# Column sums of squares moved to VectorE adds in a two-layer trunk kernel, and two reordered weight steps

## The chip, the cores and the metric

The kernel runs on 1 core of one Trainium2 chip. The metric is the time of the whole program on the device in microseconds (us), the median over runs.

## The reference, cut to what matters

The reference computes two layers on x of 1024 tokens by 1024 channels, all in float32. Each layer is a mixer sub-layer and a channel mixer, and each of these reads its input through an RMS norm:

```python
def rms_norm(x, g):
    y = xf * lax.rsqrt(jnp.mean(xf * xf, axis=-1, keepdims=True) + EPS)
...
        h = modulate(rms_norm(x, norm1_g[l]), sh1, sc1)
        x = x + g1 * mixer_sublayer(h, ...)
        h = modulate(rms_norm(x, norm2_g[l]), sh2, sc2)
        f = swiglu(h, ...) if l % 2 == 0 else moe_swiglu(h, ...)
        x = x + g2 * f
```

shift, scale and gate (`sh`, `sc`, `g`) come from `silu(c) @ ada_w[l] + ada_b[l]`. So there are four norms: the first of layer 0 reads the input x; the other three ("the later norms") read an x that the kernel has just updated.

## The kernel before, in words

x is kept transposed: a tile of 128 channels (partitions) by 1024 tokens, eight such tiles k = 0 to 7, each in two halves of 512 tokens. A norm's mean of squares over channels is therefore a sum over the partitions of eight tiles. The kernel squares a 128x512 tile on ACT and lets TensorE multiply it with a 128x128 matrix of ones; eight such column sums accumulate in a PSUM bank for each half. These matmuls are plain float32, and the trace shows each as two records of 128x512. ACT takes the square root and DVE the reciprocal.

The large products use a split: weight and activation are each a rounded part (`hi`) and its remainder (`lo`), and `mm3` (L257 to L261) issues three matmuls for one product. A weight block goes by DMA (SP's queue) into `w_raw`, ACT rounds it to `w_hi` (`round_w`), and POOL subtracts to get `w_lo` (`rest_w`). Two buffers alternate. All engines are written out by hand as five instruction streams for each phase, with semaphores between them; a barrier ends each phase. The phases in order are, for a layer: front (first norm and input projections), attention, back (gates, branch products, then w_o), and the channel mixer (dense in layer 0; route, expert, combine in layer 1).

**Back phase, w_o part** (L1311 to L1331 on TensorE): eight blocks j = NGATE to NGATE+7, each two half-blocks of 24 matmuls of 128x512. DVE adds each half-block to x (L1567, "residual"), ACT squares it (`x_square`, L1397), TensorE sums it (`x_sum`, L1286). The sum of block k's half stands behind the half-block of block k+1, so 14 of a layer's 16 sums are issued inside the w_o loop and two behind it. The roots (L1414) are the last work of the phase. ACT's stream is `round_w(j)`, then the squares of block j-2. TensorE's next half-block into the same bank waits for the residual (`added`).

**Dense phase** (L1573): for each half of the tokens a lap of 22 "up" steps (w1 and w3, 48 matmuls a step) and 8 "down" blocks (w2) of three parts each (24, 24 and 18 matmuls). Beside each part DVE multiplies and reduces a piece of the next layer's `ada_w` (`ada_part`), which TensorE adds up with a small matmul (L1752). After the third part DVE adds the block to x (L1807), ACT squares it (L1654) behind the rounding of a later part, and TensorE sums it (`total`, L1718): the total of block j-1 stands behind block j, and the last total behind the loop.

**Front phase of layer 1**: SP issues `load(0)`, the eight tiles of x (tile k for k of 4 or more waits until tile k-4 has landed), `load(1)`, then small parameters and the rope tables. ACT issues `round_w(0)`, `round_w(1)` and then the h_hi roundings (L622). DVE's stream is `invert(0)`, then for n = 0 to 15 `scale(n)` (L730) and `rest(n-1)` (L738), with `invert(1)` ahead of `scale(8)`. TensorE's first block waits for `rest(k)` at each k.

**Front phase of layer 0 (the opening)**: DVE forms four parts of the ada product (`ada_part`, L815 to L819, semaphore `added`), TensorE sums them, and DVE then makes shift and scale and enters the same stream of `scale` and `rest`. ACT has rounded weight blocks 0 and 1 by then, and POOL subtracts them (L652) as soon as they are rounded. The first norm of layer 0 sums its squares on TensorE too (L522); the change leaves that one.

Of the kernel before, what the change touches and what calls it, by code (L numbers as in the profile page):

```python
# [31 lines left out]
P = 128  # L32
# [317 lines left out]
def front_phase(nc, m, a, l):  # L350
# [44 lines left out]
    with phase(nc, *names) as (block, s):  # L395
# [6 lines left out]
        def _(sp):  # L402
# [30 lines left out]
            if not first:  # L433
                load(1)
# [127 lines left out]
        def _(act):  # L562
# [53 lines left out]
            for j in range(2):  # L616
                round_w(j)
            for half in range(NHALF):
                for k in range(KT):
                    n = KT * half + k  # L620
                    act.wait_ge(s.scaled, n + 1)
# [27 lines left out]
        def _(pool):  # L649
# [15 lines left out]

            for j in range(3):
                rest_w(j)
# [368 lines left out]
def back_phase(nc, m, a, l):  # L1036
# [31 lines left out]
    x_sq = [m.place(f"x_sq{l}{b}", [P, HALF], F32, at) for b, at in enumerate((R + 138 * KB, R + 194 * KB))]  # L1068
# [14 lines left out]
    with phase(nc, "raw0", "raw1", "br0", "br1", "hi_ready", "lo_ready", "halves", "prods", "sig", "gated", "summed", "m_hi", "m_lo",  # L1083
               "x_in0", "x_in1", "added", "stored", "x_squared", "x_summed", "x_root",
# [79 lines left out]
        def _(pe):  # L1164
# [121 lines left out]
            def x_sum(k, half):  # L1286
                pe.wait_ge(s.x_squared, 2 * k + half + 1)
                if k == 0:
                    pe.wait_ge(s.r_root, 2)
                pe.matmul(m.ps[:, 6 + half, :], cst[:, K_ONE:K_ONE + P], x_sq[half][:, :], start=(k == 0), stop=(k == KT - 1)  # L1290
                          ).then_inc(s.x_summed, 1)

# [19 lines left out]
            for j in range(NGATE, NBACK):  # L1312
                b = j % 2
                pe.wait_ge(s.lo_ready, j + 1)
                for half in range(NHALF):
# [12 lines left out]
                    if j > NGATE:  # L1328
                        x_sum(j - NGATE - 1, half)
            for half in range(NHALF):  # L1330
                x_sum(KT - 1, half)  # L1331

        @block.scalar
        def _(act):
# [63 lines left out]
            def x_square(k, half):  # L1398
                act.wait_ge(s.added, 2 * k + half + 1)
                if k:  # L1400
                    act.wait_ge(s.x_summed, 2 * k + half - 1)
                act.activation(x_sq[half][:, :], m.x[:, k, toks[half]], ACT.Square).then_inc(s.x_squared, 1)
# [9 lines left out]
            for half in range(NHALF):  # L1412
                act.wait_ge(s.x_summed, 2 * KT - 1 + half)
# [4 lines left out]
        def _(dve):  # L1418
# [136 lines left out]
            if ada:  # L1555
# [4 lines left out]
                dve.wait_ge(s.folded, 2)  # L1560
            dve.wait_ge(s.x_in0, 16 * 6)
            for k in range(KT):
                if k == 6:
                    dve.wait_ge(s.x_in1, 16 * 2)
                for half in range(NHALF):
                    dve.wait_ge(s.halves, 2 * (NGATE + k) + half + 1)
                    dve.scalar_tensor_tensor(out=m.x[:, k, toks[half]], in0=m.ps[:, half, :], scalar=m.small[:, G1 + k:G1 + k + 1],  # L1567
                                             in1=m.x[:, k, toks[half]], op0=ALU.mult, op1=ALU.add).then_inc(s.added, 1)


def dense_phase(nc, m, a, l):
# [8 lines left out]
    sq = [m.place(f"f_sq{l}{b}", [P, HALF], F32, m.R + (176 + 6 * b) * KB) for b in range(2)]  # L1580
# [16 lines left out]
    with phase(nc, "squared", "summed", "root", "inv", "scaled", "hi", "lo", "raw0", "raw1", "hi_ready", "lo_ready", "mm_done",  # L1597
# [50 lines left out]
        def _(act):  # L1648
            def square(half, j):
                n = KT * half + j  # L1650
                act.wait_ge(s.added, n + 1)
                if n >= 2:
                    act.wait_ge(s.summed, n - 1)
# [902 lines left out]
```

## Time and profile before

| | |
|---|---|
| median of 3 runs | 5590.35 us (5587.02 to 5594.34) |
| the profiled execution's own time | 5590.09 us |
| its span | 5588.0 us |
| mean granted TensorE clock | 0.976 of full speed |
| TensorE busy | 5298.8 us, 95% of the span |
| VectorE busy | 2731.7 us, 49% |
| ScalarE busy | 1809.6 us, 32% |
| GpSimd busy | 757.4 us, 14% |

The profile shows one execution. PE is TensorE's matmul stream, PEld its weight loads, DVE VectorE, ACT ScalarE, POOL GpSimd, SP the engine whose queue issues the DMAs. Times in a timeline count from the start of the span. "[5.60 <-PE banks L261]" behind an instruction says that its engine sat idle for 5.60 us before it and what ended that. "x2" is two instructions merged into one row, whose duration is then that of both. L numbers are lines of the kernel before.

### The profile page before, as it was taken

To read this page: it belongs to the slowest core of one execution; us is meant where nothing else is said; L and a number is where in the kernel's file an instruction comes from. 1 tells how busy PE (TensorE), PEld (TensorE's weight loads), DVE (VectorE), ACT (ScalarE), POOL (GpSimd) and SP (SyncE) were. 2 spreads that over 40 slices of the span, in tenths; PEclk is the share of its full clock that TensorE was granted. 3 is DMA by queue.
4 is the path that set the end of the run, shared out by engine and by line. 5 is a ranking of instruction groups with operands and counts; after the bars stand their busy time and mean duration, and the time that the engine had idled before them with its cause. 6 is when DMAs were issued, how large, how long until landed. Compare 5 with 4: busy or idle time off the path is not lost. (4 is left out here: it accounts for less than half of the span.)

```text
span 5588.0 us, 71451 instructions
## 1 busy us (share of the span) xinstructions
PE 5298.8 (95%) x29668; PEld 4435.1 (79%) x29669; DVE 2731.7 (49%) x2494; ACT 1809.6 (32%) x1615; POOL 757.4 (14%) x329
## 2 busy tenths in 40 slices
PE   7998999999999899899995999999999999999995
PEld 5676667778788667676774989999899998898985
DVE  7344257333524632623323545445575457854566
ACT  3113121132222220412112333334463336643354
POOL 1411111134444232021111000000000000000001
PEclk9999999999999899999997999999999999999997
DMA  5211124333635512021124555555595558965578
GB/s 178 79 46 51 38 77 114 110 94 109 189 95 144 181 59 67 20 61 46 43 94 161 190 194 194 190 188 195 201 333 189 187 197 304 354 220 183 193 248 301
DMA packets 810515, 854.53 MB, mean 153 GB/s; under 512 B 19250, under 2 KB 732082, under 8 KB 809906
## 3 DMA queue, kind: packets, MB, share of 16 engines
q1 hardware_dynamic: 802274, 820.18, 45.2%
q0 software_dynamic: 4608, 16.78, 0.8%
q10 hardware_dynamic: 3408, 14.68, 0.8%
q8 instruction: 127, 2.08, 0.2%
q14 instruction: 98, 0.80, 0.0%
HBM read 793.90 MB, written 57.67 MB: 152 GB/s over the span
## 5 line engine op out<-in xcount | busy, mean ns | idle before, releaser
L259 PE MATMUL banks<-h_hi,w_hi 128*128 128x512 f32 x2432 | 993.6, 409 | 76.2 <-DVE h_lo L738 34.1
L259 PE MATMUL banks<-e_x_hi,e_w_hi 128*128 128x256 f32 x3584 | 1016.2, 284 | 14.5 <-DVE e_w_lo L2233 12.2
L260 PE MATMUL banks<-e_x_lo,e_w_hi 128*128 128x256 f32 x3584 | 1015.3, 283 | 0.0
L261 PE MATMUL banks<-e_x_hi,e_w_lo 128*128 128x256 f32 x3584 | 1015.1, 283 | 0.0
L260 PE MATMUL banks<-h_lo,w_hi 128*128 128x512 f32 x2432 | 957.0, 394 | 0.0
L261 PE MATMUL banks<-h_hi,w_lo 128*128 128x512 f32 x2432 | 956.8, 393 | 0.0
L2233 DVE TENSOR_TENSOR e_w_lo<-e_raw,e_w_hi 128x2048 fp32r<-128x2048 f32 x340 | 764.1, 2285 | 192.4 <-ACT e_w_hi L2171 190.7
L2171 ACT ACTIVATE e_w_hi<-e_raw 128x2048 fp32r<-128x2048 f32 x340 | 647.3, 1911 | 503.9 <-PE banks L261 491.4
L259 PEld LDWEIGHTS banks<-e_x_hi,e_w_hi 128*128 128x128 f32 x3584 | 689.1, 192 | 17.3 <-DVE e_w_lo L2233 14.0
L260 PEld LDWEIGHTS banks<-e_x_lo,e_w_hi 128*128 128x128 f32 x3584 | 689.1, 192 | 0.1
L261 PEld LDWEIGHTS banks<-e_x_hi,e_w_lo 128*128 128x128 f32 x3584 | 689.1, 192 | 0.0
L259 PEld LDWEIGHTS banks<-h_hi,w_hi 128*128 128x128 f32 x2432 | 462.2, 190 | 227.6 <-issue 59.8
L260 PEld LDWEIGHTS banks<-h_lo,w_hi 128*128 128x128 f32 x2432 | 463.3, 191 | 103.3 <-issue 12.9
L261 PEld LDWEIGHTS banks<-h_hi,w_lo 128*128 128x128 f32 x2432 | 462.4, 190 | 100.1
L2378 DVE TENSOR_TENSOR e_w_lo<-e_raw,e_w_hi 128x2048 fp32r<-128x2048 f32 x168 | 382.4, 2290 | 252.2 <-ACT e_w_hi L2178 252.1
L2178 ACT ACTIVATE e_w_hi<-e_raw 128x2048 fp32r<-128x2048 f32 x168 | 321.9, 1916 | 371.9 <-PE banks L261 371.9
L259 PE MATMUL banks<-e_w_hi,e_hid_hi 128*128 128x512 f32 x1120 | 436.8, 390 | 0.0
L261 PE MATMUL banks<-e_w_hi,e_hid_lo 128*128 128x512 f32 x1120 | 435.8, 389 | 0.0
L260 PE MATMUL banks<-e_w_lo,e_hid_hi 128*128 128x512 f32 x1120 | 435.8, 389 | 0.0
L253 POOL TENSOR_TENSOR w_lo<-w_raw,w_hi 128x1024 fp32r<-128x1024 f32 (+1 forms) x136 | 326.0, 2398 | 465.0 <-ACT w_hi L248 465.0
L2355 DVE TENSOR_TENSOR e_act<-e_act,banks 128x512 f32<-128x512 f32 (+1 forms) x168 | 100.4, 598 | 590.0 <-PE banks L261 550.3
L1150 POOL TENSOR_TENSOR w_lo<-w_raw,w_hi 128x1024 fp32r<-128x1024 f32 x80 | 191.5, 2394 | 1212.3 <-ACT w_hi L1339 1212.3
(307 smaller groups left out, 7043.3 us busy)
## 6 DMA issues: line engine op xcount, KB each, us to landing
e_raw<-in_moe_w_dram SPq DMA_DIRECT2D x510, 1024.0 KB, 5.9
w_raw<-in_ffn_w_dram SPq DMA_DIRECT2D x120, 512.0 KB, 3.9
w_raw<-in_w_in_dram SPq DMA_DIRECT2D x108, 512.0 KB, 4.1
f_ada_raw<-in_ada_w_dram SPq DMA_DIRECT2D x48, 512.0 KB, 5.0
g_ada_raw<-in_ada_w_dram SPq DMA_DIRECT2D x32, 512.0 KB, 4.1
e_io<-row_scratch SPq DMA_DIRECT2D x13, 1024.0 KB, 7.3
x_scratch<-x_res SPq DMA_DIRECT2D x24, 512.0 KB, 2.9
row_scratch<-stage SPq DMA_DIRECT2D x24, 512.0 KB, 2.6
```

What stands on the lines that cost most here:

```text
L253: pool.tensor_tensor(m.w_lo[b][:, 0:kt, :], m.w_raw[b][:, 0:kt, :], m.w_hi[b][:, 0:kt, :].bitcast(F32), ALU.subtract).then_inc(s.lo_ready, 1)
L259: pe.matmul(out, wh, rh, start=first, stop=False)
L260: pe.matmul(out, wh, rl, start=False, stop=False)
L261: return pe.matmul(out, wl, rh, start=False, stop=last)
L1150: pool.tensor_tensor(m.w_lo[j % 2][:, :, :], m.w_raw[j % 2][:, :, :], m.w_hi[j % 2][:, :, :].bitcast(F32), ALU.subtract).then_inc(s.lo_rea ...
L2171: act.activation(flat(w_hi[u]), flat(raw[n % RING]), ACT.Copy).then_inc(s.hi_ready, 1)
L2178: act.activation(flat(w_hi[c % 4]), flat(raw[n % RING]), ACT.Copy).then_inc(s.hi_ready, 1)
L2233: eng.tensor_tensor(flat(w_lo[u]), flat(raw[n % RING]), flat(w_hi[u]).bitcast(F32), ALU.subtract).then_inc(lo_sem[u], 1)
L2355: dve.tensor_tensor(act_t[h][:, 0:width], act_t[h][:, 0:width], m.ps[:, 2 + h, 0:width], ALU.mult).then_inc(s.hid, 1)
L2378: dve.tensor_tensor(flat(w_lo[c % 4]), flat(raw[n % RING]), flat(w_hi[c % 4]).bitcast(F32), ALU.subtract).then_inc(s.lo2, 1)
```

## The change: what it does, and the diff

In the back phases of both layers and in the dense phase, the square of the first tile goes into an accumulator, each later square into a scratch tile, and a new DVE operation `pile` adds it (128x512, float32, SBUF to SBUF). One float32 matmul with the ones for each half then takes the column sum of the accumulator. In the dense phase the sum of the first half is issued behind the first up step of the second half. In layer 1's front phase the load of the second weight block is issued behind x's fourth tile, and its rounding ahead of the sixth h_hi. In layer 0's front phase POOL waits for the four ada parts ahead of its first subtraction. The lists of semaphore names change with it (left out here).

```diff
@@ front_phase, sync @@
                         sp.wait_ge(x_in[k % 4], 16)
                     sp.dma_start(m.x[:, k, :], a.xs[P * k:P * k + P, :]).then_inc(x_in[k % 4], 16)
-            if not first:
-                load(1)
+                    if k == 3:
+                        load(1)
@@ front_phase, scalar @@
-            for j in range(2):
-                round_w(j)
+            round_w(0)
+            if first:
+                round_w(1)
             for half in range(NHALF):
                 for k in range(KT):
                     n = KT * half + k
+                    if not first and n == 5:
+                        round_w(1)
                     act.wait_ge(s.scaled, n + 1)
@@ front_phase, gpsimd @@
+            if first:
+                pool.wait_ge(s.added, NB)
             for j in range(3):
                 rest_w(j)
@@ back_phase @@
-    x_sq = [m.place(f"x_sq{l}{b}", [P, HALF], F32, at) for b, at in enumerate((R + 138 * KB, R + 194 * KB))]
+    x_acc = [m.place(f"x_acc{l}{b}", [P, HALF], F32, at) for b, at in enumerate((R + 138 * KB, R + 194 * KB))]
+    x_sq = [m.place(f"x_sq{l}{b}", [P, HALF], F32, R + at * KB) for b, at in enumerate((136, 140))]
@@ back_phase, tensor @@
-            def x_sum(k, half):
-                pe.wait_ge(s.x_squared, 2 * k + half + 1)
-                if k == 0:
-                    pe.wait_ge(s.r_root, 2)
-                pe.matmul(m.ps[:, 6 + half, :], cst[:, K_ONE:K_ONE + P], x_sq[half][:, :], start=(k == 0), stop=(k == KT - 1)
-                          ).then_inc(s.x_summed, 1)
...
-                    if j > NGATE:
-                        x_sum(j - NGATE - 1, half)
+            pe.wait_ge(s.r_root, 2)
             for half in range(NHALF):
-                x_sum(KT - 1, half)
+                pe.wait_ge(s.x_piled, 2 * (KT - 2) + half + 1)
+                pe.matmul(m.ps[:, 6 + half, :], cst[:, K_ONE:K_ONE + P], x_acc[half][:, :], start=True, stop=True).then_inc(s.x_summed, 1)
@@ back_phase, scalar @@
                 act.wait_ge(s.added, 2 * k + half + 1)
-                if k:
-                    act.wait_ge(s.x_summed, 2 * k + half - 1)
-                act.activation(x_sq[half][:, :], m.x[:, k, toks[half]], ACT.Square).then_inc(s.x_squared, 1)
+                if k >= 2:
+                    act.wait_ge(s.x_piled, 2 * (k - 2) + half + 1)
+                act.activation((x_sq if k else x_acc)[half][:, :], m.x[:, k, toks[half]], ACT.Square).then_inc(s.x_squared, 1)
@@ back_phase, vector @@
+            def pile(k, half):
+                dve.wait_ge(s.x_squared, 2 * k + half + 1)
+                if k >= 2:
+                    dve.wait_ge(s.x_piled, 2 * (k - 2) + half + 1)
+                dve.tensor_tensor(x_acc[half][:, :], x_acc[half][:, :], x_sq[half][:, :], ALU.add).then_inc(s.x_piled, 1)
...
                                              in1=m.x[:, k, toks[half]], op0=ALU.mult, op1=ALU.add).then_inc(s.added, 1)
+                    if k >= 2:
+                        pile(k - 1, half)
+            for half in range(NHALF):
+                pile(KT - 1, half)
@@ dense_phase @@
-    sq = [m.place(f"f_sq{l}{b}", [P, HALF], F32, m.R + (176 + 6 * b) * KB) for b in range(2)]
+    sq, acc = (m.place(f"f_{n}{l}", [P, HALF], F32, m.R + at * KB) for n, at in (("sq", 176), ("acc", 182)))
@@ dense_phase, scalar @@
                 act.wait_ge(s.added, n + 1)
-                if n >= 2:
-                    act.wait_ge(s.summed, n - 1)
-                act.activation(sq[n % 2][:, :], x_t[n % 2][:, :], ACT.Square).then_inc(s.squared, 1)
+                if j == 0 and half:
+                    act.wait_ge(s.summed, 1)
+                if j >= 2:
+                    act.wait_ge(s.piled, (KT - 1) * half + j - 1)
+                act.activation((sq if j else acc)[:, :], x_t[n % 2][:, :], ACT.Square).then_inc(s.squared, 1)
...
                 act.wait_ge(s.hid, FT * half + f + 1)
+                if half and f == 0:
+                    act.wait_ge(s.piled, KT - 1)
@@ dense_phase, tensor @@
-            def total(half, j):
-                n = KT * half + j
-                pe.wait_ge(s.squared, n + 1)
-                pe.matmul(m.ps[:, 6 * (1 - half), :], cst[:, K_ONE:K_ONE + P], sq[n % 2][:, :], start=(j == 0), stop=(j == KT - 1)
-                          ).then_inc(s.summed, 1)
+            def total(half):
+                pe.wait_ge(s.piled, (KT - 1) * (half + 1))
+                pe.matmul(m.ps[:, 6 * (1 - half), :], cst[:, K_ONE:K_ONE + P], acc[:, :], start=True, stop=True).then_inc(s.summed, 1)
...
                     up(half, f)
+                    if half and f == 0:
+                        total(0)
                 for j in range(KT):
                     down(half, j)
-                    if j:
-                        total(half, j - 1)
-                total(half, KT - 1)
+                if half:
+                    total(half)
@@ dense_phase, vector @@
                 dve.wait_ge(s.silu, n + 1)
+                if half and f == 1:
+                    dve.wait_ge(s.summed, 1)
...
+            def pile(half, j):
+                dve.wait_ge(s.squared, KT * half + j + 1)
+                if j >= 2:
+                    dve.wait_ge(s.piled, (KT - 1) * half + j - 1)
+                dve.tensor_tensor(acc[:, :], acc[:, :], sq[:, :], ALU.add).then_inc(s.piled, 1)
...
                     for q in range(NP):
                         ada_part(half, NP * j + q)
+                    if j >= 2:
+                        pile(half, j - 1)
                     residual(half, j)
+                pile(half, KT - 1)
```

## Rows read from the trace of the kernel before

**Rows 1.** The page: busy time of each engine, its share of the span and instructions.

```profile
PE 5298.8 (95%) x29668; PEld 4435.1 (79%) x29669; DVE 2731.7 (49%) x2494; ACT 1809.6 (32%) x1615; POOL 757.4 (14%) x329
```

**Rows 2.** Stretches: length, busy PE, PEld, DVE, ACT, POOL, PEclk, DMA, GB/s.

```profile
1039.40:1121.90 82.50, 82.50 (x340) 63.45 (x339) 9.76 (x13) 12.41 (x18) 11.99 (x5) 1.00 0.16 58
1416.89:1433.45 16.56, 16.56 (x76) 13.44 (x76) 11.45 (x7) 3.49 (x5) 7.25 (x3) 1.00 0.75 216
1905.50:1917.00 11.50, 0.00 (x0) 0.00 (x0) 3.85 (x3) 1.06 (x1) 2.34 (x1) 0.50 1.04 401
```

**Rows 3.** Timeline, DVE, layer 1's w_o blocks: start, us, engine, instruction.

```profile
2876.90 0.75 DVE L1567 SCALAR_TENSOR_TENSOR x_res<-banks,small,x_res 128x512 f32<-128x512 f32 x1 [4.62 <-PE banks L261]
2882.34 0.75 DVE L1567 SCALAR_TENSOR_TENSOR x_res<-banks,small,x_res 128x512 f32<-128x512 f32 x1 [4.69 <-PE banks L261]
2888.69 0.75 DVE L1567 SCALAR_TENSOR_TENSOR x_res<-banks,small,x_res 128x512 f32<-128x512 f32 x1 [5.60 <-PE banks L261]
...
2964.85 0.75 DVE L1567 SCALAR_TENSOR_TENSOR x_res<-banks,small,x_res 128x512 f32<-128x512 f32 x1 [5.59 <-PE banks L261]
```

**Rows 4.** Timeline, DVE, the dense stage's w2 blocks, first half.

```profile
1401.19 0.75 DVE L1807 SCALAR_TENSOR_TENSOR f_x<-banks,small,f_x 128x512 f32<-128x512 f32 x1 [3.32 <-PE banks L261]
...
1416.89 0.75 DVE L1807 SCALAR_TENSOR_TENSOR f_x<-banks,small,f_x 128x512 f32<-128x512 f32 x1 [4.17 <-PE banks L261]
```

**Rows 5.** Groups by form: one 128x512 sum or difference of two SBUF tiles on DVE.

```profile
L1791 DVE TENSOR_TENSOR hid<-f_hid,hid 128x512 fp32r<-128x512 f32 x44 | 30.5, 692 | 1.5
```

**Rows 6.** Timeline, all engines, end of layer 0's back phase.

```profile
1121.98 0.75 DVE L1567 SCALAR_TENSOR_TENSOR x_res<-banks,small,x_res 128x512 f32<-128x512 f32 x1 [5.59 <-PE banks L261]
1123.18 0.63 ACT L1402 ACTIVATE x_sq<-x_res 128x512 f32<-128x512 f32 x1 [5.99 <-PE banks L1290]
1123.82 1.28 ACT L1414 ACT_TABLE_LOAD   x1
1125.12 1.27 ACT L1414 ACTIVATE norm_root<-banks,const 128x512 f32<-128x512 f32 x2
1123.86 1.13 PE L1290 MATMUL banks<-x_sq,const 128*128 128x512 f32 x2 [0.20 <-ACT x_sq L1402]
```

**Rows 7.** Timeline, POOL and ACT: turn of the dense halves, and its end.

```profile
1518.69 4.67 POOL L253 TENSOR_TENSOR w_lo<-w_raw,w_hi 128x1024 fp32r<-128x1024 f32 x2 [9.70 <-ACT w_hi L248]
...
1899.30 0.63 ACT L1654 ACTIVATE f_sq<-f_x 128x512 f32<-128x512 f32 x1 [9.96 <-DVE f_x L1807]
1901.15 0.69 ACT L1658 ACTIVATE norm_rstd<-banks,const 128x512 f32<-128x512 f32 x1 [1.22 <-PE banks L1721]
```

**Rows 8.** Timeline, DVE, ACT and POOL, layer 1's first norm.

```profile
1908.30 3.31 DVE L730 SCALAR_TENSOR_TENSOR np_tmp<-x_res,small,norm_rstd 128x512 f32<-128x512 f32 x2 [2.26 <-DMA x_res<-x_scratch]
...
1921.38 2.33 DVE L738 SCALAR_TENSOR_TENSOR h_lo<-np_tmp,small,h_hi 128x512 fp32r<-128x512 f32 x1 [9.78 <-ACT h_hi L622]
...
1931.58 3.34 DVE L720 RECIPROCAL norm_rstd<-norm_rstd 128x512 f32<-128x512 f32 x1
...
1935.63 0.74 DVE L738 SCALAR_TENSOR_TENSOR h_lo<-np_tmp,small,h_hi 128x512 fp32r<-128x512 f32 x1
...
1919.68 1.06 ACT L567 ACTIVATE w_hi<-w_raw 128x1024 fp32r<-128x1024 f32 x1 [11.70 <-DMA w_raw<-in_w_in_dram]
...
1920.82 2.35 POOL L652 TENSOR_TENSOR w_lo<-w_raw,w_hi 128x1024 fp32r<-128x1024 f32 x1 [10.42 <-ACT w_hi L567]
```

**Rows 9.** Timeline, DVE and POOL, the opening of layer 0.

```profile
40.49 4.69 DVE L817 SCALAR_TENSOR_TENSOR ada_part<-ada_w,small,ada_part 128x512 f32<-128x512 f32 x6
...
46.39 8.83 DVE L817 SCALAR_TENSOR_TENSOR ada_part<-ada_w,small,ada_part 128x512 f32<-128x512 f32 x6
...
57.97 0.17 DVE L288 TENSOR_TENSOR small<-banks,small 128x16 f32<-128x16 f32 x1 [1.96 <-PE banks L543]
...
58.38 1.42 DVE L730 SCALAR_TENSOR_TENSOR np_tmp<-x_res,small,norm_rstd 128x512 f32<-128x512 f32 x2
...
47.22 5.09 POOL L652 TENSOR_TENSOR w_lo<-w_raw,w_hi 128x1024 fp32r<-128x1024 f32 x2 [46.79 <-ACT w_hi L567]
```

More of the change, by code:

```diff
@@ L1083, in back_phase @@
     with phase(nc, "raw0", "raw1", "br0", "br1", "hi_ready", "lo_ready", "halves", "prods", "sig", "gated", "summed", "m_hi", "m_lo",
-               "x_in0", "x_in1", "added", "stored", "x_squared", "x_summed", "x_root",
+               "x_in0", "x_in1", "added", "stored", "x_squared", "x_piled", "x_summed", "x_root",
                "gelu", "g_squared", "g_summed", "g_root", "g_inv", "g_normed", "g_turned", "vt_in", "mixed", "biased", "y2",
@@ L1412, in _ @@
             for half in range(NHALF):
-                act.wait_ge(s.x_summed, 2 * KT - 1 + half)
+                act.wait_ge(s.x_summed, half + 1)
                 act.activation(m.rstd2[:, half, :], m.ps[:, 6 + half, :], ACT.Sqrt, bias=cst[:, K_EPS:K_EPS + 1], scale=1.0 / D
@@ L1596, in dense_phase @@
     INV_STEP, H_STEP = 6, 7
-    with phase(nc, "squared", "summed", "root", "inv", "scaled", "hi", "lo", "raw0", "raw1", "hi_ready", "lo_ready", "mm_done",
+    with phase(nc, "squared", "piled", "summed", "root", "inv", "scaled", "hi", "lo", "raw0", "raw1", "hi_ready", "lo_ready", "mm_done",
                "silu", "hid", "hid_hi", "hid_lo", "x0", "x1", "added", "st0", "st1",
@@ L1651, in square @@
                 act.wait_ge(s.added, n + 1)
-                if n >= 2:
-                    act.wait_ge(s.summed, n - 1)
-                act.activation(sq[n % 2][:, :], x_t[n % 2][:, :], ACT.Square).then_inc(s.squared, 1)
+                if j == 0 and half:
[3 more added lines that the diff above has]
+                act.activation((sq if j else acc)[:, :], x_t[n % 2][:, :], ACT.Square).then_inc(s.squared, 1)
             def root(half):
-                act.wait_ge(s.summed, KT * half + KT)
+                act.wait_ge(s.summed, half + 1)
                 act.activation(m.rstd0[:, half, :], m.ps[:, 6 * (1 - half), :], ACT.Sqrt, bias=cst[:, K_EPS:K_EPS + 1], scale=1.0 / D
```

## The prediction, made before the changed kernel was run

> **What bounds the kernel now.** I read the page's busy times first: TensorE works for 95% of the span and no other engine for more than 49% [rows 1]. Shares don't say what a matmul fewer is worth, so next I read the stages that the change touches. In the w_o blocks the stretch is all TensorE: 82.50 of 82.50 us busy at full granted clock, DVE 9.76, ACT 12.41, POOL 11.99; in a dense w2 block it is 16.56 of 16.56 with DVE at 11.45 [rows 2]. Last, the timelines of the seams between phases, where TensorE idles and a chain over ACT, DVE, POOL and the DMAs sets the time. So sums inside a loop are paid on TensorE, and the rest on those chains.
>
> **Part 1, sums out of the w_o loops.** The distance of two residuals on DVE is one half-block of TensorE. Before the first sum it is 5.44 us (2882.34 - 2876.90), with a sum in it 6.35, and it stays so to the last: 13 x 6.35 from 2882.34 is 2964.85 [rows 3]. A sum costs 0.91. Of 14 sums issued in the loop the last stands behind the last half-block, beside the residual: 13 count. Two layers: 26 x 0.91 = **-23.7 us**.
>
> What comes in their place is one `pile` on DVE for each, 0.69 us by the nearest row of two SBUF inputs [rows 5]. It stands behind the residual that frees TensorE's bank, and DVE sits idle 5.6 us ahead of each residual, so it is free there. POOL's w_lo shares the stretch, and either may wait for the other by up to 2.4 us; both have over 3 us to spare. ACT's square now waits for the pile behind the same residual, and a weight rounding queued behind the square has most of a 10.9 us block left.
>
> **Part 2, the ends of the back phases.** Now: last residual 1121.98, square 1123.18 (held until then by the sum before it), table load to 1125.10, two roots to 1126.39 [rows 6]. After: residual to 1122.7, pile(6) to 1123.4, square to 1124.0 with pile(7, 0) beside it, pile(7, 1) to 1124.75, its sum of 1.13 (the two sums overlap by a little) to 1126.0, root to 1126.7. That is +0.3 each, **+0.6** for both. Bounds: 0, where the old wait of 0.45 hid more, and +2.0, three piles in a row with nothing given back.
>
> **Part 3, the dense phase.** A w2 block takes 15.70 us without a sum (1401.19 to 1416.89) [rows 4] and 16.56 with one [rows 2]: 0.86. Seven totals are issued inside a half's loop, of which the last stands beside the last residual; six count, in two halves: 12 x 0.86 = **-10.3**. The eighth of the first half is hidden today: TensorE has to wait there for the two weight blocks on which POOL works from 1518.7 to 1523.4 [rows 7]. Its successor stands behind an up step, where nothing idles: **+0.9**. DVE has 11.45 of a block's time in use [rows 2] and the pile makes it 12.1 of 15.7; it goes in front of the residual, where DVE idles 4.2 us [rows 4]. The new waits of silu and `hidden` on buffers are for work that ended a step earlier: nothing. At the end of the phase the chain square, total, root (1899.30 to 1901.84) [rows 7] gets a pile between square and total: **+0.7**, between 0.3 (if the store of x, issued with the square, is what the barrier waits for) and 1.2.
>
> **Part 4, layer 1's first norm.** DVE's first two scales end at 1911.61. The first `rest` comes only at 1921.38, since ACT's h_hi stands behind `round_w(1)`, which starts when its weights land, 1919.68 [rows 8]. With the rounding behind five h_hi, the first h_hi follows the first scale, and the first rest starts at about 1911.7. From the first rest to the eighth, on which TensorE's first block ends, it was 14.25 us (1921.38 to 1935.63), with one POOL subtraction that held DVE up (2.33 for 0.74) and one reciprocal (3.34) in it; without them seven tiles take 9.3, 1.33 each. The subtraction for block 1 now falls a few tiles later into the same stretch, so I keep 14.25: the eighth rest at 1925.95, 9.7 earlier.
>
> Of the queue: `load(1)` moves past four loads of x. At 401 GB/s [rows 2] a 512 KB load takes 1.3 us. x's first tile lands at 1908.3 [rows 8], so the last, eight loads later with the weights among them, at about 1918.8; DVE wants it at 1912.4 + 5 x 1.33 = 1919.0. That is tight but met. The worst case has a bound too: the same bytes had landed by 1919.68, so scale(7) starts then at the latest, and three operations of half a tile's 1.33, the reciprocal and a POOL hold of up to its whole 2.35 put the eighth rest at 1927.4: gain 8.2. The rounding of 1.06 in ACT's stream may delay the sixth rest by some tenths. I take **-9.2**, ends -8.2 and -9.7. The parameter loads behind keep their place and have 10 us and more.
>
> **Part 5, the opening.** Six ada operations take 4.69 us alone and 8.83 beside POOL's two subtractions (5.09) [rows 9]: 4.14 lost. After the change the parts end at 56.01 - 4.14 = 51.87; POOL then works to 56.96, while DVE's scale is ready at 58.38 - 4.14 = 54.24. Overlap 2.72, of which DVE lost 0.81 per us before: 2.2 lost, **-1.9** net. Ends: -4.1 (no hold) and -1.4 (held for all of it). TensorE's first block wants w_lo(0) at 54.4 and the first rest after 57, so DVE sets its start, as before.
>
> The Trainium skill ("SBUF — State Buffer", Who interferes with whom) has a rule on this: a DVE instruction with two SBUF inputs and a GpSimd one that reads SBUF exclude each other, and the later one is blocked for all of the earlier. By it this part would be 1.4 rather than 1.9, and the sum 0.5 us smaller. The rule speaks against the new piles as well, whose cover is stated above.
>
> **The sum.** -23.7 + 0.6 - 10.3 + 0.9 + 0.7 - 9.2 - 1.9 = -42.9 us. The profiled execution took 5590.09 by its own time (span 5588.0 and 2.1 around it), 0.3 below the median of 5590.35. So 5590.35 - 42.9 = 5547.4, given as 5547.
>
> **Rivals.**
> A. *The second weight block lands late after all.* If the DMA engines serve the open loads side by side, it may land with the last of them, 1919.68. The sixth h_hi then follows its rounding, the sixth rest starts at 1921.4, and two scales, a rest, the reciprocal and a hold later comes the eighth, at about 1929.5: 6 us instead of 9.2. With the opening at its lower end the sum is 3.7 less, 5551. For it: x's tiles and this load share one stretch of 401 GB/s [rows 2]. Against: x's first tile landed in its order, long before the last [rows 8].
> B. *Another engine paces the dense blocks.* Without the sum, the chain of ada loads and DVE pieces sets the block: part 3 gives nothing (-10.3 lost), 5558. For: DVE would be in use for 77% of a block. Against: the block of 15.70 had no sum and ran at TensorE's pace [rows 4].
> C. *A wait takes the sums' place; slower.* In the w_o loop pile(k-1) stands on DVE ahead of the next half's residual and waits for a square that stands on ACT behind `round_w`, which itself waits for TensorE to end a block. If that square came later than the next residual is due, over 5.44 us behind its own residual, TensorE would lose a half-block in each of the 14 blocks: 14 x 5.44 = 76, so 5590.35 - 42.9 + 76 = 5624. Against: the square starts 1.2 us behind its residual [rows 6], and its rounding waits only for the block that has just ended.
> D. *The sums were hidden.* Nothing but parts 4 and 5 comes, less the new chain pieces of 2.2: 5581. Against: 6.35 against 5.44.
>
> **How the numbers follow.** Forecast 0.81, A 0.10, B 0.06, D 0.02, C 0.01. With all terms at their best ends the forecast is 5544, with all at their worst 5551, where A lies too. The range adds 3 us below and 5 above, since the runs of before spread over 7 and the rules on who holds the port were read from few rows: 5541 to 5556; B, C and D lie outside. A measurement here tells about 0.2%, 11 us, from no change: faster is the forecast, A and B, 0.97; same 0.02 (D); slower 0.01 (C).
>
> **What the profile after would show.** Residuals 5.44 us apart all through w_o in both layers, w2 blocks 15.70 apart, TensorE full in both. 14 piles a layer in back and 14 in dense at about 0.69. The first h_hi of layer 1 right behind the first scale, the eighth rest some 14 us behind the first, and x's last tile no longer than tenths awaited. In the opening six ada operations at 4.69 in the fourth part, and a stretched first scale. Wrong would be: a residual with idle time put down to a pile or a square; POOL's w_lo stretched beyond what TensorE leaves, or ACT's rounding of layer 1's second block waiting for its load.

## The result, and the profile after

The changed kernel takes 5525.52 us (median of 4 runs, 5524.56 to 5527.48) against 5588.69 (4 runs, 5586.77 to 5594.34): ratio 0.9886, 95% interval 0.9874 to 0.9899, about 63 us faster. 5547 with a range of 5541 to 5556 was forecast. The sign was right, the amount was not: the kernel is 15 us below the low end, and no rival lies there either. The profiled execution took 5524.56 by its own time. One execution of the last experiment (e12) took 6323 us at a granted clock of 0.785, where all others have 0.972 to 0.979, and is left out.

The page's span, busy times, and the two queues that carry instructions (packets, MB, share):

```profile
span 5522.5 us, 71355 instructions
PE 5249.8 (95%) x29584; PEld 4413.2 (80%) x29585; DVE 2749.0 (50%) x2536; ACT 1810.1 (33%) x1615; POOL 756.5 (14%) x329
q8 instruction: 106, 1.74, 0.1%
q14 instruction: 42, 0.34, 0.0%
```

Against [rows 1] TensorE has 49 us less and VectorE 17 more. The page of before has for the two queues:

```profile
q8 instruction: 127, 2.08, 0.2%
q14 instruction: 98, 0.80, 0.0%
```

Twenty-one packets on q8 and 56 on q14 are gone with the change. At 0.2% of the DMA engines that looked like nothing, and it is the clue to what the forecast lacked.

**The stretches that the change edits** went as drawn. VectorE's timeline in layer 1's w_o blocks, then in layer 0's w2 blocks:

```profile
2848.50 0.75 DVE L1572 SCALAR_TENSOR_TENSOR x_res<-banks,small,x_res 128x512 f32<-128x512 f32 x1 [4.69 <-PE banks L261]
2853.94 0.75 DVE L1572 SCALAR_TENSOR_TENSOR x_res<-banks,small,x_res 128x512 f32<-128x512 f32 x1 [4.69 <-PE banks L261]
2859.38 0.75 DVE L1572 SCALAR_TENSOR_TENSOR x_res<-banks,small,x_res 128x512 f32<-128x512 f32 x1 [4.69 <-PE banks L261]
2860.05 0.68 DVE L1564 TENSOR_TENSOR x_acc<-x_acc,x_sq 128x512 f32<-128x512 f32 x1
2864.82 0.75 DVE L1572 SCALAR_TENSOR_TENSOR x_res<-banks,small,x_res 128x512 f32<-128x512 f32 x1 [4.09 <-PE banks L261]
...
1399.01 0.75 DVE L1821 SCALAR_TENSOR_TENSOR f_x<-banks,small,f_x 128x512 f32<-128x512 f32 x1 [4.11 <-PE banks L261]
1410.45 0.69 DVE L1828 TENSOR_TENSOR f_acc<-f_acc,f_sq 128x512 f32<-128x512 f32 x1
1414.71 0.75 DVE L1821 SCALAR_TENSOR_TENSOR f_x<-banks,small,f_x 128x512 f32<-128x512 f32 x1 [3.57 <-PE banks L261]
```

The residuals stay 5.44 us apart with a pile between them, where [rows 3] has 6.35; the w2 blocks are 15.70 apart (16.56 in [rows 2]), and each residual still waits for TensorE.

**The expert phase**, of which no line was changed, is where the rest came from. It works in a loop over items, each up to 256 rows (tokens) of one expert; an item with at most 128 rows takes the narrow branch of the loop, another the wide one. An item is counted here from ScalarE's first rounding of its rows. The first starts at 3048.3 before and 3003.9 after, 44.4 us earlier: up to here the total of 42.9 holds (its parts less well, see below). From the first item's start to the last's it is 2425.2 us before and 2405.6 after, 19.6 less, and the stretch behind is 1.5 shorter: 44.4 + 19.6 + 1.5 = 65.5, the difference of the spans. From one start to the next a long item (the wide branch) takes 241.3 before and 240.2 after, a narrow one 169.5 and 165.6. VectorE's waits in that phase, before and then after (total us, times, longest):

```profile
DVE e_act L2355 <- PE banks L261: 550.3, 140, 8.6
DVE e_act L2355 <- issue: 28.7, 4, 8.3
```

```profile
DVE e_act L2378 <- PE banks L261: 571.9, 148, 6.0
```

"issue" is a wait for nothing that the profile shows. One of the four, on VectorE's timeline of before, with what it does to TensorE on the second line:

```profile
3316.78 0.69 DVE L2355 TENSOR_TENSOR e_act<-e_act,banks 128x512 f32<-128x512 f32 x1 [8.33 <-issue]
...
3321.35 0.38 PE L259 MATMUL banks<-e_x_hi,e_w_hi 128*128 128x256 f32 x1 [0.84 <-DVE e_w_lo L2233]
```

After the change the same operation comes as soon as TensorE allows:

```profile
3275.44 0.69 DVE L2378 TENSOR_TENSOR e_act<-e_act,banks 128x512 f32<-128x512 f32 x1 [5.24 <-PE banks L261]
```

And the instruction queues' packets from the first item's start to the last's, before, then after:

```profile
q8 instruction: 25, 0.41, 0.1%
q14 instruction: 59, 0.48, 0.1%
```

```profile
q8 instruction: 6, 0.10, 0.0%
q14 instruction: 5, 0.04, 0.0%
```

The items are a loop. In the kernel after, the packets in it are about one fetch of its instructions (six of 16.4 KB on q8, where TensorE's loop has 1730 instructions); in the kernel before there are four times as many on q8 and twelve times on q14.

### The profile page after: what moved, and what is told of

Same layout as the page of the kernel before. It is cut to its first block and busy times, and to the rows that moved or that the text cites. A ratio compares the mean times of both kernels' runs of the same rounds, so it can differ in the third digit from the quotient of the medians.

```text
span 5522.5 us, 71355 instructions
## 1 busy us (share of the span) xinstructions
PE 5249.8 (95%) x29584; PEld 4413.2 (80%) x29585; DVE 2749.0 (50%) x2536; ACT 1810.1 (33%) x1615; POOL 756.5 (14%) x329
## 3 DMA queue, kind: packets, MB, share of 16 engines
q1 hardware_dynamic: 802274, 820.18, 45.7%
q8 instruction: 106, 1.74, 0.1%
## 5 line engine op out<-in xcount | busy, mean ns | idle before, releaser
L259 PEld LDWEIGHTS banks<-e_x_hi,e_w_hi 128*128 128x128 f32 x3584 | 688.9, 192 | 11.1 <-DVE e_w_lo L2256 10.9
```

Of the source, the lines that this page charges most:

```text
L259: pe.matmul(out, wh, rh, start=first, stop=False)
```

## The experiments

The theory: the change makes VectorE's stream 78 instructions longer ahead of the expert loop (counted in the compiled program; the trace shows them as 42 operations and 36 waits) and TensorE's 170 shorter, so the loops begin at other places within the blocks in which instructions are fetched. Rivals: the 20 us are the clock's, another engine's, or come from the data path that was changed. The tool is a wait that always holds already, put where its engine idles: it changes no result and no order, and only lengthens the stream (two such waits make one instruction in most places; 166 of them made 78).

**Move VectorE's loop alone.** The edit in the kernel before, in `hidden` of the dense phase (166 waits over its 44 calls):

```diff
                 dve.tensor_tensor(hid_lo[f], ...).then_inc(s.hid_lo, 1)
+                for _ in range(166 * (FT * half + f + 1) // (NHALF * FT) - 166 * (FT * half + f) // (NHALF * FT)):
+                    dve.wait_ge(s.hid, 2)
```

> The kernel before with 166 waits on VectorE that never hold (hid at 2, which it has from the start), spread over its 44 hidden blocks of the dense phase. They make 78 instructions, so VectorE's loop of the expert phase begins at its instruction 2058, as in the changed kernel, and not at 1980; TensorE's stays at 11621 and ScalarE's at 1581. Theory (the 20 us more than forecast come from where VectorE's expert loop lies in its instruction stream: it is fetched again every round): the expert phase becomes 20 us shorter, to intervals of 240.2 us for the long items instead of 241.3, the 8.3 us waits of VectorE at its line 2355 go, and the time is 5589 - 20 = 5569 (5565 to 5573). Rival (TensorE's or ScalarE's place in their streams, or the clock, or the layer-1 data path): 5589, intervals as before. Rival (the waits themselves cost): over 5589.

Measured 5570.38 us (6 runs) against 5591.04 for the kernel before beside it: 20.7 us less, ratio 0.9968 (0.9955 to 0.998, which is 11 to 25 us), by idle instructions alone. The packets of the first item to the last's:

```profile
q8 instruction: 25, 0.41, 0.1%
q14 instruction: 5, 0.04, 0.0%
```

Q14 is down to the 5 of the changed kernel and q8 where it was. No wait of VectorE in the items is put down to "issue" any more. The long items take 240.2 us, but two of them, in the later half, 241.6.

The same edit with 354 waits in the changed kernel puts the loop back:

> The changed kernel with 354 such waits on VectorE (178 instructions), so that its expert loop begins at 2236 = 1980 + 256, the place of before within a block of 256 instructions; everything else as in the changed kernel. Theory (VectorE's place modulo 256 decides): the expert phase gets its 20 us back, long items at 241.3 us, total 5525.5 + 20 = 5545 (5541 to 5550). Rival (another engine or the clock): 5525.5.

Measured 5549.34 us (4 runs), long items 241.1 to 241.4, 59 packets on q14 in the items, and 45.7 us of "issue" in front of VectorE's `e_act`: 24 us lost, the other direction of the same effect.

**Which block size.** The waits now stand at the head of the expert phase, beside the wait for its first rows (100 of them, 256 in the second kernel):

```diff
             dve.sem_inc(s.y_in, 1)
+            for _ in range(100):
+                dve.wait_ge(s.hid, 2)
```

> The changed kernel with 100 waits on VectorE that never hold, at the head of the expert phase (50 instructions, beside its wait for the first rows): its expert loop begins at 2108 = 1980 + 128. The DMA table gives 8 KB to a packet of the instruction queue that VectorE shares (0.34 MB in 42), so blocks of 128 instructions, if one has 64 bytes. Theory (the place within a block of 128 decides): slow as in the kernel before, about 95 packets on that queue, long items 241.2 us, 5525.5 + 21 to 24 = 5547 to 5549. Rival (blocks of 256): the place is one that neither kernel has had, and nothing says that it is slow; 5525.5 if it is not.

> The same with 256 waits (128 instructions), loop at 2186 = 2058 + 128. Theory (blocks of 128): as the changed kernel, about 42 packets, 5525.5 (within 3). Rival (blocks of 256): another place than the changed kernel's, and so a loss of up to 24 us.

Measured 5550.57 us with 50 instructions more and 5528.34 with 128 more. A shift by 128 changes nothing but 2.9 us in the first item (175.2 for 172.3, the waits themselves), and one by 50, which is before's place plus 128, brings all of it back (25 us, a little over what was expected). So a shift by 128 instructions leaves the place as good as it was, which agrees with the 8 KB of a packet on q14. A period of 64 would fit these shifts as well; none of the runs rules it out.

**The other engines.**

```diff
                 act.activation(act_t[f % 2][:, :], ..., ACT.Silu).then_inc(s.silu, 1)
+                if half == 0 and f < 5:
+                    for _ in range(2):
+                        act.wait_ge(s.hid, 2)
...
                     pe.wait_ge(s.lo, KT * half + KT)
+                for _ in range(2):
+                    pe.wait_ge(s.hid, 2)
```

> The changed kernel with waits that never hold on TensorE (44 instructions, two waits ahead of each up block) and ScalarE (5 instructions), so that both engines' expert loops begin where they did before (11621 and 1581), and VectorE's stays where the change put it (2058). Theory (VectorE's place alone): 5525.5, at most 1 to 2 us more for the 44 instructions on TensorE. Rival (TensorE's or ScalarE's place): the 20 us come back, 5545.

Measured 5572.38 us (6 runs), 47 more than the changed kernel, far outside both. The expert loop did it, on TensorE itself:

```profile
3258.19 0.39 PE L261 MATMUL banks<-e_w_hi,e_hid_lo 128*128 128x512 f32 x1
3264.88 0.58 PE L259 MATMUL banks<-e_x_hi,e_w_hi 128*128 128x256 f32 x1 [6.30 <-issue]
```

Once in each long item TensorE stands for 6.3 to 6.7 us with nothing to wait for, and then works at a lower clock for some us. The six us behind this stall and the six after those (length, then PE, PEld, DVE, ACT, POOL busy, then the granted clock, DMA share, GB/s):

```profile
3264.88:3270.88 6.00, 6.00 (x33) 6.00 (x34) 4.49 (x2) 1.93 (x2) 0.00 (x0) 0.61 1.04 324
3270.88:3276.88 6.00, 6.00 (x51) 5.90 (x51) 0.00 (x0) 3.68 (x3) 0.00 (x0) 1.00 0.93 292
```

33 matmuls where 51 fit: of the 9 us by which these items are longer (249 us), over 2 are the clock and the rest the stall. The queue q8 has 73 packets in the items:

```profile
q8 instruction: 73, 1.20, 0.2%
q14 instruction: 5, 0.04, 0.0%
```

My expectation said that the 44 instructions put TensorE's loop where it lay before. They did not: I had counted a matmul as one instruction. The page counts 84 matmuls fewer for 42 sums taken away, so an fp32 sum is executed as two, each with its weight load, and counts four; counted so, before and after differ by 170, not 44, and this kernel has a place of its own. That q14 stays at 5 clears ScalarE, whose place was before's here, and in e1 too.

With the count mended, TensorE's loop alone, by waits where it waits anyway, for the router's input and for the expert phase's first rows:

```diff
             pe.wait_ge(s.w_in, 32)
+            for _ in range(80):
+                pe.wait_ge(s.w_in, 32)
...
             pe.sem_inc(s.mm_done, 4)
+            for _ in range(260):
+                pe.wait_ge(s.mm_done, 4)
```

> The changed kernel with TensorE's expert loop moved by 170 instructions to 159 modulo 256, where it lies in the kernel before and in e1; VectorE's stays at 2058. Theory (in e1 two items were 241.6 instead of 240.2 us, so TensorE's place of before costs 2.8 us, and VectorE's the rest of the 20): about 127 packets on TensorE's queue, two or three items of 241.6 us, 5525.5 + 2.8 and at most 3 for waits that do not fit: 5528 to 5532. Rival (the place as counted does not decide): 240.2 us throughout and 106 packets.

Measured 5537.31 us (5 runs), above the 5528 to 5532 expected, since the waits cost 8 us and not at most 3: they made TensorE stand 46.9 us for the rows where it is 38.9 otherwise; of the rest, 3.5 are two long items of 242.0 and 241.9 (in each TensorE stands 1.4 to 1.5 us with nothing to wait for), with 25 packets on q8, as before and in e1. So of before's expert phase TensorE's place costs 3 us and VectorE's 17; the stretch behind, where TensorE waits 15.8 us for `c_diag` before, 16.0 in e2 and 15.8 in e5, but 13.6 in every kernel with VectorE's loop at the other place, goes with VectorE's place too.

| kernel | VectorE, mod 128 | TensorE, mod 256 | q14, q8 packets in all | first to last item, us | time, us |
|---|---|---|---|---|---|
| before | 60 | 159 | 98, 127 | 2425.2 | 5588.7 |
| e1 | 10 | 159 | 42, 127 | 2408.5 | 5570.4 |
| e2 | 60 | 245 | 100, 106 | 2426.8 | 5549.3 |
| e5 | 60 | 245 | 99, 106 | 2424.4 | 5550.6 |
| e6 | 10 | 245 | 43, 106 | 2408.5 | 5528.3 |
| after | 10 | 245 | 42, 106 | 2405.6 | 5525.5 |
| e11 | 10 | 159 | 42, 127 | 2410.0 | 5537.3 |
| e9 | 10 | 245 | 42, 107 | 2406.7 | 5555.4 |
| e10 | 10 | 245 | 42, 107 | 2405.9 | 5542.7 |
| e4 | 10 | 245 | 43, 106 | 2405.6 | 5534.7 |
| e12 | 10 | 245 | 42, 106 | 2405.9 | 5525.7 |
| e3 | 10 | 33 | 43, 173 | 2451.6 | 5572.4 |
| e7 | 10 | 45 | 42, 174 | 2456.1 | 5616.0 |
| e8 | 10 | 17 | 42, 107 | 2406.6 | 5550.7 |

The places are where the loop begins in the compiled stream, from an origin of my own; the differences between kernels agree with the instructions that the traces show. The time of e12 is the median of three executions.

**Each part undone.** The front phase's part (load and rounding of the second weight block as in before; no count changes):

```diff
-                    if k == 3:
-                        load(1)
+            if not first:
+                load(1)
...
-            round_w(0)
-            if first:
-                round_w(1)
+            for j in range(2):
+                round_w(j)
...
-                    if not first and n == 5:
-                        round_w(1)
```

> The changed kernel without the part for layer 1's first norm: the second weight block's load is issued ahead of x again, and its rounding stands ahead of the eight first halves. No engine's instruction count changes. Theory as forecast (the sixth to eighth rests come 9.2 us earlier by the change): 5525.5 + 9 = 5534.5 (5533.7 to 5535.2). Rival (the traces show a gain of 7.8 us in this phase, of which 3.8 are lost again before attention's end): 5529 to 5533.

Measured 5534.73 us (4 runs), 9.2 more. That it is the forecast to the tenth is chance: the four runs lie between 5529.17 and 5537.11, and the profiled ones of the two kernels are 4.6 apart.

The whole function of the back phase is before's again (14 column sums more in each layer, no piles), with waits as above at the head of the expert phase (396 on TensorE, 104 on VectorE), first with a place of TensorE's that I had miscounted:

> The changed kernel with the whole back phase of before (all 16 column sums of the w_o stretch in each layer), and waits that never hold at the head of the expert phase, in TensorE's 38 us wait for the rows and VectorE's beside it, so that TensorE's expert loop keeps its place modulo 256 instructions (a matmul counted as two, its weight load and its product) and VectorE's is at 2058. Forecast of the parts: 26 sums at 0.91 us less two ends at 0.3 = 23.1, so 5548.6 (5547.5 to 5550). Rival D (the sums were hidden): 5525.5. Rival (part of the 20 us is the sums' doing after all): over 5552.

Measured 5616.0 us (4 runs). Sums cannot explain it, the table does: TensorE's loop at 45, items of 250 us. 5525.5 + 23.1 for the sums + 50.5 in the items + 15.7 by which the idle waits outlast the wait for the rows (54.4 for 38.7) is 5614.8. With the place right (284 waits on TensorE, 80 of them at the router):

> As e7 (the whole back phase of before in the changed kernel), with TensorE's place now counted as the instructions are executed: an fp32 product takes two matmuls and two weight loads (the page counts 84 matmuls fewer for the 42 column sums taken away), so each counts four. By that count TensorE's expert loop of the changed kernel lies at 245 modulo 256, before's and e1's at 159, e3's at 33 and e7's at 45 (the two that lost 6.3 us in every long item), e8's at 17. Here it is at 245 again, VectorE's at 2058. Theory: no fetch stalls, about 107 packets on TensorE's queue, long items 240.2 us; the time is the forecast's 5525.5 + 23.1 = 5548.6 (5547 to 5551). Rival D (sums hidden): 5525.5. Rival (e7's 5616 came from the sums, not from the place): over 5600.

Measured 5555.36 us (5 runs), items 240.2. TensorE's wait for the rows, 5.1 longer than its 38.7:

```profile
3037.84 2.58 PE L2268 MATMUL banks<-const,e_io 128*128 128x128 f32 x11 [43.80 <-issue]
```

Less these 5.1 it is 5550.3, so the part is worth 24.8 (forecast 23.1), from five runs that lie between 5549.7 and 5562.8. The 5555.36 itself is above the 5547 to 5551 expected.

The dense phase's function as before, with 456 and 52 waits, then 400 and 52 with TensorE's split between router and rows (e8 happened to get a harmless place, but too many waits):

> The changed kernel with the whole dense phase of before, and waits that never hold at the head of the expert phase so that both expert loops keep their places. Forecast: 12 x 0.86 - 0.9 - 0.7 = 8.7, so 5534.2 (5533.5 to 5535.5). Rival (the dense phase gained 10 to 12 us by the traces, since the granted clock was 0.93 instead of 1.00 in a stretch of before): up to 5537 if that clock belongs to the sums and comes back with them, else as forecast.

> As e8 with TensorE's loop at 245 modulo 256; its waits that never hold are split between the router's wait (40 instructions) and the wait for the rows (160), since e8 showed 228 of them at the second place to take 57.7 us where the wait was 39.0, 18.7 us too long. Theory: 5534.2 plus 1 to 3 for waits that do not fit (5533.5 to 5538), long items 240.2 us. Rival: the dense phase gives more than the 8.7 us forecast, 5537 to 5541.

Measured 5550.66 and 5542.65 us; less the 18.7 and 11.4 by which the waits outlast the wait for the rows, 5532.0 and 5531.3: the part is worth 6 rather than 8.7, though runs of e10 from 5539.5 to 5545.6 hardly tell the two apart. Both medians are above what was expected, and above their rivals, because of the waits.

The opening:

```diff
-            if first:
-                pool.wait_ge(s.added, NB)
             for j in range(3):
                 rest_w(j)
```

> The changed kernel without the wait that puts the opening's remainders behind its parts. VectorE's and TensorE's places unchanged. Forecast of that part: 1.9 us (1.4 to 4.1); the trace shows 2.5 us at the first rest. So 5527.4 to 5528.0. Rival (the part gained nothing that lasts, since the front phase's stretches at a lower clock swallow it): 5525.5.

The three times are 5524.60, 5525.69 and 5531.12 us: they can't tell 2 us. Its timeline can, at the spot: the first rest starts at 59.53 us, and at 57.39 in the changed kernel, 2.1 earlier. Whether that lasts to the end is not shown.

## Why the prediction was wrong, and where it was right

**The step that failed** is in the sum: it took each edit's own stretch and let all else stand, so the expert phase and what follows it entered at nothing, without a reason, where the runs show about 20 us. The prediction read "the stages that the change touches" and no other. But the change lengthens VectorE's stream and shortens TensorE's, and the expert loop behind them is sensitive to where it lies. That is 20 us, shown from both sides by e1 and e2 (20.7 and 24) and split by e11. Nothing about the sums or piles enters: e1 has none of the change. The forecast's total for the parts, set on a kernel with the changed kernel's places, comes out: e1's 5570.4 less TensorE's 3 less 42.9 is 5524.5; measured 5525.5. That the place fell well was luck: e3 is the changed kernel with 44 idle instructions of TensorE's and loses 47.

It could have been suspected from the trace of before: 59 packets of instructions in a loop of 292 on VectorE, and 28.7 us of "issue" in front of one of its operations. How much the change would turn it, and which way, no row told, so such a case belongs in the range as a rival to either side.

**That the total came out so well is partly luck too.** Stretch by stretch, from VectorE's timelines of the two profiled executions:

| start of | before | after | gained since the row above |
|---|---|---|---|
| layer 0, first w_o residual | 1031.02 | 1026.19 | 4.8 |
| layer 0, last w_o residual | 1121.98 | 1105.28 | 11.9 |
| first w2 residual of half 0 | 1401.19 | 1383.31 | 1.2 |
| last w2 residual of half 0 | 1516.25 | 1493.51 | 4.9 |
| first w2 residual of half 1 | 1783.46 | 1758.71 | 2.0 |
| last w2 residual of half 1 | 1898.52 | 1868.82 | 5.0 |
| layer 1, first w_o residual | 2871.53 | 2837.69 | 4.1 |
| layer 1, last w_o residual | 2964.85 | 2919.22 | 11.8 |
| first item | 3048.3 | 3003.9 | -1.2 |

The rows of w_o and w2 are what the forecast said. The first row gains 4.8 where 1.9 was forecast, the turn of the dense halves 2.0 where it should lose 0.9, and the stretch with layer 1's norm 4.1 where 8.5 was due. These are stretches in which the granted clock changes from kernel to kernel: the eleven kernels that share the changed kernel's code up to layer 0's first w_o residual reach it between 1023.1 and 1031.9.

The Trainium skill ("Runtime: NRT & Kernel Launch", Instruction fetch mechanics) says that instructions are prefetched in sequence, in blocks of 16 KiB (256 instructions), into a memory that holds 512 of them (2048 on TensorE), and that a taken branch to a target outside the current window of two blocks stalls for a fetch. Stalls at a loop are what the runs show, the 6.3 us of e3 among them. The size agrees for TensorE (1.74 MB in 106 packets, 16.4 KB) but not for VectorE: its packets have 8 KB (0.34 MB in 42), and e6 finds a shift of 128 instructions harmless. By the page's sizes VectorE's loop of 292 instructions would fit into 512 and TensorE's of 1730 (both branches of an item) into 2048. At the places 245 and 17 TensorE's does (5 to 7 packets in the items); at 33 and 45 it is fetched over and over, and so is VectorE's at the place 60. What rule tells the bad places from the good ones is open.

**Part 1** (-23.7). From the first residual to the last, layer 0 took 90.9 to 91.0 us in the four kernels with the sums in the loop and 79.1 in the changed one, 11.9 less (up to 80.0 in others, with stretches at a lower clock); layer 1 93.3 in before and e1 (93.0 in e7 and e9) and 81.5 in the changed kernel, 11.8 less: 23.7. Right.

**Part 2** (+0.6). Layer 0: last residual to the last root's end 4.77 us, and 4.41 by [rows 6]: +0.36, as drawn. Layer 1 lost 2.1 up to the router's first product. TensorE stands 2.14 us for the last pile, the granted clock falls, and the two sums take 3.33 us for 1.95; in e4, the same code, it doesn't fall. Of the ten profiled executions with this end, layer 1's last residual to the last root's end takes 6.1 to 6.5 us in seven and 4.78 in three (e4, e8, e12); before has 4.12. The windows (length, then PE, PEld, DVE, ACT, POOL busy, then the clock), of the changed kernel, then the stretch of e4 that answers to the last:

```profile
2911.30:2918.30 7.00, 7.00 (x32) 5.81 (x31) 1.35 (x2) 0.63 (x1) 0.00 (x0) 1.00 0.01 2
2918.30:2921.30 3.00, 0.88 (x4) 0.39 (x4) 1.95 (x3) 0.63 (x1) 0.00 (x0) 1.00 0.17 70
2921.30:2925.30 4.00, 3.33 (x4) 0.91 (x4) 0.69 (x1) 2.58 (x3) 0.00 (x0) 0.57 0.19 79
```

```profile
2926.40:2930.40 4.00, 1.95 (x4) 0.65 (x4) 0.94 (x2) 2.66 (x3) 0.29 (x1) 1.00 0.20 81
```

0.57 is the lower of the two levels, 1.2 GHz, for most of the stretch. The forecast priced the wait and not this: +0.4 and +2.1 are 2.5 for both layers, over the bound of +2.0. Up to the first item 1.2 of layer 1's 2.1 are left.

**Part 3** (-8.7 net). The eight w2 blocks of a half take 110.2 and 110.1 us from residual to residual where they took 115.1: 9.8 less of the 10.3, the rest at a lower clock (e7 and e9 have 109.9 in the first half, the full 5.16 less). The total behind the up step costs 0.8 against e10, which has before's dense phase (265.2 for 264.4 from the last w2 residual of one half to the first of the other), but before itself takes 267.2 there. The first 20 us of that turn have a granted clock of 0.83 in before, 0.91 after and 1.00 in e10; the last 20 have 0.92, 1.00 and 0.91:

```profile
1756.25:1776.25 20.00, 17.66 (x73) 14.14 (x72) 11.40 (x10) 3.45 (x4) 6.78 (x4) 0.92 0.46 128
```

```profile
1733.51:1753.51 20.00, 17.66 (x80) 14.33 (x79) 11.37 (x10) 3.45 (x4) 6.61 (x3) 1.00 0.47 132
```

The end costs 0.7, on these two rows of ScalarE:

```profile
1869.61 0.63 ACT L1665 ACTIVATE f_sq<-f_x 128x512 f32<-128x512 f32 x1 [9.96 <-DVE f_x L1821]
1872.18 0.69 ACT L1669 ACTIVATE norm_rstd<-banks,const 128x512 f32<-128x512 f32 x1 [1.94 <-PE banks L1733]
```

2.57 from square to root, and 1.85 in [rows 7]. So 8.3 in its own stretches against e10 and 11.1 against before; by the times of e8 and e10 only 6 arrive. From the phase's last residual to the first of layer 1's w_o the changed kernel takes 968.9 us and e10 964.0, and by windows of 40 us its clock is 0.91 and 0.93 in two where e10's is 1.00. Executions with the same front phase and dense phase differ by nearly as much there (965.4 in e11, 968.9 in the changed kernel). But scatter alone is a weak account: the nine kernels with the changed dense phase and layer 1's changed front phase have 965.4 to 969.9, and the two with before's dense phase, e8 and e10, 964.5 and 964.0. So some 4 us of the gain seem to be lost behind the dense phase; by what path is open.

**Part 4** (-9.2). Rival A is out: the rounding of the second block runs between two h_hi without a wait (columns as above, ScalarE):

```profile
1887.48 0.72 ACT L625 ACTIVATE h_hi<-np_tmp,small 128x512 fp32r<-128x512 f32 x1 [0.84 <-DVE np_tmp L735]
1888.11 1.05 ACT L567 ACTIVATE w_hi<-w_raw 128x1024 fp32r<-128x1024 f32 x1
1889.06 0.70 ACT L625 ACTIVATE h_hi<-np_tmp,small 128x512 fp32r<-128x512 f32 x1
```

The first rest and the eighth, on VectorE:

```profile
1883.14 0.75 DVE L743 SCALAR_TENSOR_TENSOR h_lo<-np_tmp,small,h_hi 128x512 fp32r<-128x512 f32 x1
...
1898.16 0.75 DVE L743 SCALAR_TENSOR_TENSOR h_lo<-np_tmp,small,h_hi 128x512 fp32r<-128x512 f32 x1
```

15.02 us apart where I kept 14.25. The eighth rest comes 29.3 us behind the dense phase's last residual, 37.1 before and 37.2 in e4: 7.8 earlier, with the 0.7 of the new chain piece in it 8.5 for the part. By the medians 9.2. But from the dense phase's last residual to layer 1's first w_o residual it is 973.0 before, 972.9 in e4 and 968.9 after: in the profiled executions half of the gain is gone again by then.

**Part 5** (-1.9). 2.1 by the timelines of e12 and after. The first scales stretch as forecast:

```profile
51.41 4.64 POOL L655 TENSOR_TENSOR w_lo<-w_raw,w_hi 128x1024 fp32r<-128x1024 f32 x2 [50.97 <-DVE ada_part L824]
53.81 3.45 DVE L735 SCALAR_TENSOR_TENSOR np_tmp<-x_res,small,norm_rstd 128x512 f32<-128x512 f32 x2
```

The two scales take 3.45 us, where a pair takes 1.4 alone: 2.0 lost in the 2.24 that POOL still works beside them, 0.91 per us. I had taken 0.81 of 2.72. The full exclusion of the Trainium skill ("SBUF — State Buffer", Who interferes with whom) is 1 per us; this row lies halfway between the two.

**Rivals B, C and D** show nothing of themselves: each residual in the rows above waits for TensorE, and its distances are the ones without a sum.

## What to carry to other kernels

Before an edit ahead of a hardware loop, look at the instruction queues' packets inside the loop and at waits put down to "issue": if a loop that should be fetched once shows packets in every round, its time depends on where it lies, any edit upstream moves it, and an estimate needs a rival for it to either side. Test it with instructions that do nothing, placed where the engine idles, before praising or blaming the edit; two versions are compared at equal places. Count the places as executed, where an fp32 matmul is four instructions.

## What the runs showed of the hardware that was not expected

- VectorE's loop of 292 instructions costs 1.1 us a long item and 3.9 a narrow one at one place and nothing at another, and a shift by 128 instructions changes nothing; TensorE's of 1730 costs nothing at two places, 1.4 to 1.8 us in each of two items at a third and 9 to 10 us in each long item at two more.
- One fetch stall holds an engine for some us: VectorE was back 8.3 us after it went idle where the data allowed 5.2, TensorE 6.3 where it allowed none. TensorE's stall costs more than its length: the granted clock was 0.61 in the 6 us behind it.
- A wait that already holds is not free on TensorE: with 102, 130, 160, 198 and 228 idle instructions ahead of the rows (e9, e11, e10, e7, e8) it stood 43.8, 46.9, 50.1, 54.3 and 57.7 us, which is 0.11 us for each. (The expectation of e10 puts all 57.7 down to the 228; by these five, 32.6 us of it pass without them.)
- A wait of 2.1 us ahead of two sums was followed by the clock's fall to 1.2 GHz in layer 1 in seven of ten executions of the same code, and in layer 0 in none. Over a phase such stretches make 4 us between kernels with the same code there, and 9 us over the first 1030.
